# Moving the first expert's down product ahead of the second gather of slots, with an earlier load and wider table operations

## The reference, cut to what matters

```python
def hierarchical_moe(h, w_group, b_group, w_expert, b_expert, w_gate, w_up, w_down):
    ...
    weights = (g_w * e_w).reshape(-1)
    expert = (g_idx * EXPERTS_PER_GROUP + e_idx).reshape(-1)
    order = jnp.argsort(expert)
    tok = order // EXPERT_TOPK
    xs = t[tok]
    sizes = jnp.bincount(expert, length=N_EXPERTS).astype(jnp.int32)
    hid = jax.nn.silu(lax.ragged_dot(xs, w_gate, sizes)) * lax.ragged_dot(xs, w_up, sizes)
    out = lax.ragged_dot(hid.astype(xs.dtype), w_down, sizes)
    out = out * weights[order][:, None].astype(out.dtype)
    y = jnp.zeros_like(t).at[tok].add(out.astype(t.dtype))
```

## Time and profile before

| what | value |
|---|---|
| times of three runs | 1330.54, 1327.62, 1325.86 us; median 1327.62 |
| profiled execution, span | 1325.6 us (which of the runs it was isn't given; the span is all that is known of its time) |
| PE (matmul) busy | 1143.6 us, 86% |
| DVE busy | 634.0 us, 48% |
| ACT busy | 412.5 us, 31% |
| q1, the loads of SP | 335.06 MB, 66.5% of 16 engines |
| the chain that ended last | PE 68%, DMA 22%, DVE 5%, ACT 3% |
| of it, waiting for in_w_up | 21% |

### The profile page before, as it was taken

One profiled execution on the slowest core, in us unless ns is written; L12 is line 12 of the kernel. 1 busy time (PEld: TensorE's weight loads), 2 busy tenths in 40 slices (PEclk: granted clock), 3 DMA queues, 4 the chain that ended last, 5 costly groups with the idle time before them and its releaser, 6 DMA issues.

```text
span 1325.6 us, 22956 instructions
## 1 busy us (share of the span) xinstructions
PE 1143.6 (86%) x9319; PEld 922.7 (70%) x9321; DVE 634.0 (48%) x997; ACT 412.5 (31%) x519; POOL 32.7 (2%) x71
## 2 busy tenths in 40 slices
PE   9999999999989899999899999778766668567666
PEld 8998999998968899999798898653322323223222
DVE  5787877775444555446445787452221112111213
ACT  3765333324474433335333665320000000000001
POOL 0000000000000000000000000000000000000000
PEclk9999999999999999999999999878888889788889
DMA  9666988873530865550754334689999999999996
GB/s 350 218 253 223 335 300 301 301 270 127 191 128 1 286 193 188 190 190 32 136 177 143 128 134 173 260 326 417 428 430 429 428 428 430 428 429 430 428 428 257
DMA packets 99400, 362.47 MB, mean 273 GB/s; under 512 B 4160, under 2 KB 51664, under 8 KB 84112
## 3 DMA queue, kind: packets, MB, share of 16 engines
q1 hardware_dynamic: 95216, 335.06, 66.5%
q0 software_dynamic: 3984, 26.50, 5.0%
q10 hardware_dynamic: 144, 0.10, 0.0%
HBM read 360.58 MB, written 1.06 MB: 273 GB/s over the span
## 4 chain that ended last, share of the span: by engine, by line
PE 68%; DMA 22%; DVE 5%; ACT 3%; issue 2%; SPq 0%; DVEq 0%; POOL 0%; POOLq 0%; ACTq 0%
DMA wbuf<-in_w_up 21%; PE ps L1737 19%; PE ps L1672 15%; PE ps L1647 9%; PE ps L2032 7%; PE ps L1638 3%; PE ps L1656 3%; PE ps L1910 3%; PE ps L2082 2%; PE ps L1617 2%; PE ps L2052 1%; DVE parts L1057 1%; PE ps L1806 1%; DMA wbuf<-in_lru_w_in 1%; ACT parts_f L689 1%
## 5 line engine op out<-in xcount | busy, mean ns | idle before, releaser
L1737 PE MATMUL ps<-big_parts,parts 128*128 128x256 f32 x2112 | 261.6, 285 | 5.6 <-DVE big_parts L1057 5.1
L1057 DVE TENSOR_TENSOR parts<-wbuf,parts 128x2048 fp32r<-128x2048 f32 x88 | 200.1, 2289 | 136.9 <-ACT parts L799 52.3
L1737 PEld LDWEIGHTS ps<-big_parts,parts 128*128 128x128 f32 x2112 | 258.2, 194 | 7.7 <-issue 5.8
L2032 PE MATMUL ps<-wbuf,big 128*32 128x256 f32 x2176 | 167.2, 474 | 107.5 <-DMA wbuf<-in_w_up 100.1
L2032 PEld LDWEIGHTS ps<-wbuf,big 128*32 128x32 f32 x2176 | 86.2, 135 | 202.7 <-issue 94.0
L1672 PE MATMUL ps<-big_parts,parts 128*128 128x256 f32 x1344 | 166.1, 283 | 1.1 <-DVE parts_f L1261 1.1
L1672 PEld LDWEIGHTS ps<-big_parts,parts 128*128 128x128 f32 x1344 | 163.3, 192 | 1.3 <-issue 1.3
L989 ACT ACTIVATE big<-ps 128x128 f32<-128x128 f32 x33 | 9.2, 278 | 421.3 <-PE ps L2032 421.3
L1564 DVE TENSOR_TENSOR big<-big,ps 128x128 f32<-128x128 f32 x33 | 9.5, 288 | 264.1 <-ACT big L989 264.1
L1647 PE MATMUL ps<-parts_f,parts 128*128 128x256 f32 x672 | 97.2, 284 | 0.0
L1647 PEld LDWEIGHTS ps<-parts_f,parts 128*128 128x128 f32 x672 | 87.9, 192 | 0.2
(11 more groups left out here) (313 smaller groups left out, 1343.7 us busy)
## 6 DMA issues: line engine op xcount, KB each, us to landing
wbuf<-in_w_down SPq DMA_DIRECT2D x32, 2048.0 KB, 38.0
wbuf<-in_w_gate SPq DMA_DIRECT2D x31, 2048.0 KB, 32.6
wbuf<-in_w_up SPq DMA_DIRECT2D x31, 2048.0 KB, 37.1
wbuf<-in_ffn_w_in SPq DMA_DIRECT2D x44, 1024.0 KB, 11.1
wbuf<-in_w_ada POOLq DMA_DIRECT2D x24, 1024.0 KB, 8.3
wbuf<-in_ffn_w_out SPq DMA_DIRECT2D x22, 1024.0 KB, 5.1
wbuf<-in_w_in SPq DMA_DIRECT2D x10, 2048.0 KB, 8.1
wbuf<-in_attn_w_qkv SPq DMA_DIRECT2D x6, 2048.0 KB, 8.6
```

The lines of the kernel that those rows point to most:

```text
L1057: nc.vector.tensor_tensor(lo, whole, hi.bitcast(F32), ALU.subtract).then_inc(done, 1)
L1737: ins = mm(ps[:, b, d * 256:(d + 1) * 256], w[pw][:, k, d * P:(d + 1) * P], h_part_of[px][:, k], start=(k == 0 and i == 0), stop=(k == KC ...
L2032: ins = mm(at, rows, gu_place[s][:, :, k, r * P:(r + 1) * P], start=(k == 0), stop=(k == KC - 1))
```

## The change

It takes the first expert's down product from behind the second gather to ahead of it, on TensorE, and its hidden product ahead of the tables on VectorE. TensorE's wait for spread_ev goes with it, and a wait for y_ev comes into the gather. The spread products are made inside the first gate and up product, behind k = 4 and k = 6, the first of them into bank 3. gate_tile gets a place of its own, and POOL loads it directly after turned_mod. The table of further windows is made in two operations with a table of constants (full_windows, over_full), and that of row numbers in three. The memset of the last slots goes behind the first expert. The descriptor scratch of the software DMA is set to 8192 bytes.

```diff
--- before.py
+++ after.py
@@ -52,8 +52,9 @@
 
 C_ID, C_AFTER, C_BEFORE, C_ONES, C_ROT, C_STICK, C_NEG = 0, 128, 256, 384, 512, 640, 1024
 C_IOTA = 1408
-C_ROW = C_IOTA + GRP
-N_CONST = C_ROW + 1
+C_ROWS = C_IOTA + GRP
+C_FULL = C_ROWS + SEQ // WIN
+N_CONST = C_FULL + SEQ // WIN - 1
 N_ROUTE = N_GRP + N_EXP
 
 
@@ -153,6 +154,8 @@
         ada = sb("ada", [P, 48])
         gain = sb("gain", [P, 2, KC])
         small = sb("small", [P, 400])
+        gate_tile = sb("gate_tile", [P, 512])[:]
+        over_full = sb("over_full", [P, N_EXP * (SEQ // WIN - 1)])[:]
         bias36 = sb("bias36", [P, N_GRP + N_EXP])
         info = sb("info", [1, 3 * N_EXP], I32)
         turned_mod = cols[:, R_CW:R_CW + 2 * KC]
@@ -169,7 +172,8 @@
         minus_ones = cst[:, C_STICK + P:C_STICK + 2 * P]
         negm = cst[:, C_NEG:C_NEG + 384]
         iota8 = cst[:, C_IOTA:C_IOTA + GRP]
-        row_no = cst[:, C_ROW:C_ROW + 1]
+        row_of_window = cst[:, C_ROWS:C_ROWS + SEQ // WIN]
+        full_windows = cst[:, C_FULL:C_FULL + SEQ // WIN - 1]
 
         def flat(lo, n):
             return big[:, lo:lo + n]
@@ -231,7 +235,6 @@
 
             return h2_high[:, :, q // 2 * P:(q // 2 + 1) * P].rearrange("t k p -> t p k")[:, (q % 2) * (P // 2):(q % 2 + 1) * (P // 2)]
 
-        gate_tile = flat(10752, 512)
         final_row = wbuf[:, 2 * EXPERT:2 * EXPERT + D].rearrange("p (h f) -> p h f", h=2)
         part_logits = flat(5120, SEQ)
         zero_half = big_half[:, 2 * 512:2 * 512 + 512]
@@ -599,16 +602,13 @@
                 pool.dma_start(mod_dram[v].rearrange("(k p) -> p k", p=P), at, allow_slow_non_contiguous=True).then_inc(mod_stored, 16)
             pool.wait_ge(mod_stored, 48)
             pool.dma_start(turned_mod.rearrange("p (v k) -> p v k", v=2), mod_dram[0:2].rearrange("v (p k) -> p v k", k=KC)).then_inc(mod_turned, 16)
+            for h in range(2):
+                pool.dma_start(gate_tile[h * HALF_ROWS:(h + 1) * HALF_ROWS], mod_dram[2:3, h * 512:(h + 1) * 512].to_broadcast([HALF_ROWS, 512])).then_inc(gate_in, 16)
 
             pool.wait_ge(av_done, PAIRS)
             pool.dma_start(w_route, a["w_route"].rearrange("p (k n) -> p k n", k=KC)).then_inc(route_in, 16)
             pool.wait_ge(x_ready, 4 * 6)
             pool.dma_start(slot_no, a["slot_numbers"]).then_inc(slotno_in, 16)
-
-            pool.wait_ge(mod_stored, 48)
-            pool.wait_ge(spread_pe, 2)
-            for h in range(2):
-                pool.dma_start(gate_tile[h * HALF_ROWS:(h + 1) * HALF_ROWS], mod_dram[2:3, h * 512:(h + 1) * 512].to_broadcast([HALF_ROWS, 512])).then_inc(gate_in, 16)
 
             pool.wait_ge(info_ready, 1)
             n_more = pool.value_load(info[0:1, N_EXP:N_EXP + 1], min_val=0, max_val=SEQ // WIN - 1)
@@ -979,7 +979,7 @@
             nc.scalar.activation(first_silE, ps[:, 0, 0:P], ACT.Silu).then_inc(silu_done[0], 1)
             act.wait_ge(pick_ready, 2 * TC)
             act.wait_ge(spread_pe, 1)
-            nc.scalar.activation(slot_bc, ps[:, 1, :], ACT.Identity, bias=1.0).then_inc(spread_ev, 1)
+            nc.scalar.activation(slot_bc, ps[:, 3, :], ACT.Identity, bias=1.0).then_inc(spread_ev, 1)
             act.wait_ge(spread_pe, 2)
             nc.scalar.activation(weight_bc, ps[:, 2, :], ACT.Copy).then_inc(spread_ev, 1)
 
@@ -1529,23 +1529,29 @@
             ins.then_inc(spread_ready, 1)
 
             link(V.tensor_tensor(sm(32, 32), sm(32, 32), sm(START, 32), ALU.subtract))
-            link(V.tensor_scalar(sm(96, 32), sm(32, 32), float(WIN), None, ALU.is_gt))
-            for w in range(2, SEQ // WIN):
-                link(V.scalar_tensor_tensor(out=sm(96, 32), in0=sm(32, 32), scalar=float(w * WIN), in1=sm(96, 32), op0=ALU.is_gt, op1=ALU.add))
+            over_of = over_full.rearrange("p (e w) -> p e w", e=N_EXP)
+            link(V.tensor_tensor(over_of, sm(32, 32).unsqueeze(2).to_broadcast([P, N_EXP, SEQ // WIN - 1]),
+                                 full_windows.unsqueeze(1).to_broadcast([P, N_EXP, SEQ // WIN - 1]), ALU.is_gt))
+            link(V.reduce_sum(sm(96, 32), over_of, AX_X))
             V.tensor_copy(info[:, 32:64], small[0:1, 96:128]).then_inc(info_ready, 1)
             pick_half(1)
             link(V.tensor_tensor_scan(sm(128, 32), cst[:, C_ONES:C_ONES + 32], sm(96, 32), 0.0, ALU.mult, ALU.add))
             link(V.tensor_tensor(sm(128, 32), sm(128, 32), sm(96, 32), ALU.subtract))
             V.tensor_copy(info[:, 0:32], small[0:1, 0:32])
             V.tensor_copy(info[:, 64:96], small[0:1, 128:160]).then_inc(info_ready, 1)
-            for w in range(SEQ // WIN):
-                V.tensor_scalar(row_slot_t[:, w * N_EXP:(w + 1) * N_EXP], sm(START, 32), row_no, float(w * WIN + 1), ALU.add, ALU.add)
-                ins = V.tensor_scalar(row_used[:, w * N_EXP:(w + 1) * N_EXP], sm(32, 32), float(-w * WIN), row_no, ALU.add, ALU.is_gt)
-            link(ins)
-            link(V.tensor_tensor(row_slot, row_slot_t, row_used, ALU.mult))
+            dve.wait_ge(silu_done[0], 1)
+            V.tensor_tensor(first_hidE, first_silE, ps[:, 0, P:2 * P], ALU.mult).then_inc(hid_done[0], 1)
             V.memset(yE[0], 0.0).then_inc(y_ev[0], 1)
             V.memset(comb[0], 0.0).then_inc(comb_ready[0], 1)
-            V.memset(xs[:, :, SLOTS:], 0.0).then_inc(rows_end, 1)
+
+            def by_window(v):
+                return v.rearrange("p (w e) -> p w e", e=N_EXP)
+
+            every = [P, SEQ // WIN, N_EXP]
+            rows = row_of_window.unsqueeze(2).to_broadcast(every)
+            V.tensor_tensor(by_window(row_slot_t), sm(START, 32).unsqueeze(1).to_broadcast(every), rows, ALU.add)
+            link(V.tensor_tensor(by_window(row_used), sm(32, 32).unsqueeze(1).to_broadcast(every), rows, ALU.is_ge))
+            link(V.tensor_tensor(row_slot, row_slot_t, row_used, ALU.mult))
 
             def rest_of_window(q, count, at):
                 dve.wait_ge(hidT_pe[q], count + 1)
@@ -1564,8 +1570,6 @@
                 V.tensor_tensor(hidE, silE, ps[:, 0, P:2 * P], ALU.mult).then_inc(hid_done[q], 1)
                 rest_of_window(q, count, at)
 
-            dve.wait_ge(silu_done[0], 1)
-            V.tensor_tensor(first_hidE, first_silE, ps[:, 0, P:2 * P], ALU.mult).then_inc(hid_done[0], 1)
             dve.wait_ge(spread_ev, 2)
             dve.wait_ge(gate_in, 32)
             dve.wait_ge(info_ready, 2)
@@ -1574,6 +1578,7 @@
                 dve_window(1, w, nc.s_assert_within((w + 1) * N_EXP, 0, SEQ // WIN * N_EXP - 1, skip_runtime_bounds_check_because="w + 1 is less than the windows of a whole sequence"))
                 dve.wait_ge(more_done, w + 1)
             rest_of_window(0, 0, 0)
+            V.memset(xs[:, :, SLOTS:], 0.0).then_inc(rows_end, 1)
 
             with dve.Fori(1, N_EXP) as e:
                 n_more, before_more = more_windows(dve, e)
@@ -2037,10 +2042,11 @@
             for k in range(KC):
                 pe.wait_ge(gather_ev, k + 1)
                 ins = gate_up_product(k, xs[:, k, 0:WIN], 0)
+                if k in (4, 6):
+                    q = k // 2 - 2
+                    pe.wait_ge(spread_ready, 1)
+                    mm(ps[:, 3 - q, :], ones, spread[:, q], start=True, stop=True).then_inc(spread_pe, 1)
             ins.then_inc(first_gu, 1)
-            pe.wait_ge(spread_ready, 1)
-            for q in range(2):
-                mm(ps[:, 1 + q, :], ones, spread[:, q], start=True, stop=True).then_inc(spread_pe, 1)
             pe.wait_ge(zero_ready, 1)
             for b in range(4, 8):
                 mm(ps[:, b, :], zero_half[:, 0:P], zero_half, start=True, stop=False, skip_group_check=True)
@@ -2110,18 +2116,17 @@
                 pe.wait_ge(comb_ready[1], 2 * w + 2)
                 combine(1).then_inc(more_done, 1)
             nc.tensor.nop().then_inc(gu_done[0], 1)
+            pe.wait_ge(spread_ev, 2)
+            down_part(0, 0, 0, 1, first_hidE)
             pe.wait_ge(pick_ready, 2 * TC)
             for k in range(KC):
-                if k == 2:
-                    pe.wait_ge(spread_ev, 2)
-                if k == 6:
-                    pe.wait_ge(hid_done[0], 1)
+                if k == 4:
+                    pe.wait_ge(y_ev[0], 2)
                 b = (3, 1, 2, 0)[k // 2]
                 for i, (rows, c) in enumerate(((rows_high, 0), (rows_high, 1), (rows_low, 0), (rows_low, 1))):
                     ins = mm(ps[:, b, k % 2 * 256:(k % 2 + 1) * 256], rows(k, c), pick[1][:, c], start=(i == 0), stop=(i == 3))
                 ins.then_inc(gather_pe, 1)
             pe.wait_ge(gather_ev, 2 * KC)
-            down_part(0, 0, 0, 1, first_hidE)
             pe.wait_ge(info_ready, 2)
             with pe.Fori(0, (N_EXP - 2) // EXPERT_SLOTS) as j:
                 for i in range(1, EXPERT_SLOTS + 1):
@@ -2152,7 +2157,8 @@
     causal = np.where(i[None, :] <= i[:, None], 0.0, NEG)
     table[:, C_NEG:C_NEG + 384] = np.concatenate([causal, np.zeros((P, P)), causal], axis=1)
     table[:, C_IOTA:C_IOTA + GRP] = np.arange(GRP)
```

(5 more changed lines are left out.)

## The result

The changed kernel is slower: a median of 1333.98 us in 20 runs against 1327.53 us in 20 runs of the kernel before; the ratio of the two kernels, in which two disturbed executions of the changed kernel (1380 and 5278 us) don't count, is 1.0035, with a 95% interval of 1.0019 to 1.005, so +4.6 us (2.5 to 6.6). The three runs shown ahead of the prediction had nearly the same median of before (1327.62). The profiled execution after has a span of 1332.5 us, and its own time is 1334.26. The span is 6.9 us longer than the span of before. Two causes have to be kept apart in that: 4.5 us of it are there when G3 is issued (879.85 against 875.33), and 2.4 us come after (1332.5 - 879.85 = 452.6 against 1325.6 - 875.33 = 450.3).

What follows compares the result with a forecast made beforehand. The last 460 us were taken as bound by the weight stream and its holes. Old hole -2.9, gate_tile's bytes -0.8 and new hole +0.8 gave -2.9 us: from the median 1327.62 to 1324.7, range 1321.5 to 1329.9.

Steps and rivals of the forecast that it cites:

- G3: Load of expert 3's gate and up weights; its issue was forecast to stay at 875.3 us, with 0.1 either way.
- the old hole: Gap in the weight stream from 888.5 to 891.4 us, ahead of D3's bytes; forecast to close, 2.9 us gained.
- Part 1: gate_tile's loads moved far ahead of the experts: 0.8 us gained, at most 1.3, as their bytes leave the weight stream.
- Parts 2 and 3: Tables in fewer operations, and spread products inside the first product: nothing gained, with 0.1 us either way for the latter.
- Part 4: First expert's down product ahead of the gather: D3 issued earlier, 2.9 us gained, then 0.8 lost to a new hole.
- new hole of 0.8 us: Stream empty between D3's end at 892.6 and G4's bytes at 893.4; 0 if steps overlap, 2.5 at half clock.
- G4: Load of expert 4's gate and up weights, forecast to be issued at 891.8 us, with bytes from 893.4.
- D3: Load of expert 3's down weights, forecast to be issued at 880.7 us, at latest 882.4; before, at 889.78.
- I take the full clock: First expert's down product on TensorE, assumed at the 2.4 GHz level: 1.93 us, against 3.64 at half clock.
- G5: Load of expert 5's gate and up weights, forecast issued at 907.0 us, before at 909.65; no more than 0.5 lost.
- (c): Rival: VectorE's 7.79 us wait was its branch, not gate_tile, and moves with it: net +6.3, 1333.9 us; chance 0.07.
- (a): Rival: TensorE pays a code or clock stall at expert 1, priced at 4.03 us: net +1.1, 1328.7 us; chance 0.13.

Runs made afterwards that it cites:

- e1: Kernel before with only gate_tile loaded early, plus the smaller DMA scratch that makes room: ratio 0.9999 (0.9979 to 1.002), 445.8 us from G3 to the end.
- e8: Repeat of e1, the kernel before with only the early gate_tile load: ratio 0.9982 (0.996 to 1.0005), 446.4 us from G3 to the end.
- e10: Third run of e1, the kernel before with only the early gate_tile load: ratio 0.9982 (0.9963 to 1.0002), 446.4 us from G3 to the end.
- e3: Changed kernel with gate_tile's loads late again, behind spread_pe, in their own place: ratio 1.0037 (1.0017 to 1.0057).
- e2: Changed kernel with the first down product back behind the second gather: ratio 1.0004 (0.9978 to 1.0029), 445.8 us from G3 to the end.
- e11: Repeat of e2, the changed kernel with the down product back behind the gather: ratio 0.9972 (0.9955 to 0.9989), 446.1 us from G3 to the end.
- e9: Changed kernel again, unaltered, for a second profile: ratio 1.0029 (1.0012 to 1.0046), 453.7 us from G3 to the end.
- e4: Changed kernel with 26 more matmuls of zeros, 10 ahead of the down product and 16 behind the gather: ratio 1.0042 (1.0022 to 1.0062).
- e5: Kernel before with early gate_tile load, short tables and SP's release for G3 directly behind the first gate and up product: ratio 0.9983 (0.9962 to 1.0004).

## Why the prediction was wrong, point by point

I forecast 1324.7 us and 2.9 us less than before, with 1321.5 to 1329.9 as the range; it is 1333.98, 4.6 us more by the ratio.

**What bounds the kernel** was right: over the thirteen profiles of the table the stretch to the end goes with the stream's missing time, to 1 or 2 us, and the old hole and its cause (gate_tile, late) were as read. Undoing only that wait removed it in e1, e8 and e10.

**Part 1** was priced at 0.8 us, and the closing of the hole, 2.9 us, was booked under part 4. The early load does both by itself: alone it takes 3.9 to 4.7 us off the stretch (450.3 and 450.5 against 445.8, 446.4 and 446.4), a little more than the 3.7 of the two terms together. The whole time shows some 2 us of it. So the gain was right in its cause, and none of it needed the new order. The early loads landed after 3.0 us at most. The formula of the Trainium skill (DMA: Bandwidth & Descriptors, Anatomy of one DMA), 2.3 us for 128 KB, is 0.4 to 0.7 us short of the early loads, and the same loads took up to 9.1 us beside G3 in the profile of before and 5.4 in e3, where it doesn't hold.

**Parts 2 and 3** were costed at nothing, and at the end e2 and e11 show nothing against the gate load alone.

**Part 4** has the step that failed: "A **new hole of 0.8 us**", from "G4 is issued at 891.8", 16.5 us after G3. It was 21.1 and 21.0, and the hole 6.3 us. Part 4 as a whole stands in the sum with a gain of 2.1 us (-2.9 + 0.8); against the same kernel with the old order (e2, e11) it costs 6.5 to 7.9 us of the stretch. D3's issue was put at 5.4 us after G3 and came at 7.3 and 6.9. The terms, in the first profile:

- the copy: forecast 3.0 us after G3 (878.3), measured 3.2.
- "I take the full clock" for the down product, 1.93 us: it took 3.64, and 3.31 in e9. The clock fell in TensorE's pause ahead of it (2.46 us idle; the windows of 882 and 884 have 0.62 and 0.50), though I had the row of 0.66 and 0.50 beside me and named this as a bound. 1.7 us.
- the gather 5.06 instead of 4.01, its first part at the lower clock. 1.05 us.
- from ScalarE's last copy (893.15) to expert 1's product (895.42), 2.3 instead of 2.0. The two reads are in view:

```profile
L464 PEldq TENSOR_LOAD <-info x1: 319/319/319, 893.4 to 893.4; - x1
L465 PEldq TENSOR_LOAD <-info x1: 310/310/310, 894.2 to 894.2; - x1
```

- expert 1's product 5.35 instead of 3.7, and 6.51 in e9: TensorE had been idle for 3.3 us, and the clock went down again, in the first profile within the product (1.00 at 894 to 896, 0.54 at 896 to 898), in e9 ahead of it. 1.65 us.

With 0.2 for the copy and 0.3 for the reads these add up to 4.9 us, 0.3 more than the 4.6 between 16.5 and 21.1, which the rounded steps of the forecast leave. The lower clock has 1.7 + 1.05 + 1.65 = 4.4 of them; in e9 it has 4.3, divided otherwise (3.31, 4.08 and 6.51 us for the three). e4, in which the clock stayed up, bears this out up to expert 1's product. In the forecast every pause of TensorE was counted with its own length only, and most of the miss at G4 was the lower clock of the work behind the pauses. Then the hole: the bytes of D3 ran out at 896.3, 16.5 us after G3 and 0.8 earlier than I had worked out, so that it is 6.3 us wide, not 0.8. G5 added its own: expert 2's stop, 4.90 against 4.03, and a further lower clock brought some 2 us at 917 to 919, where I had allowed 0.5.

Of the **rivals**, (c) has the nearest number (1333.9) by a mechanism that didn't happen, and (a) the nearest mechanism: a hole before G4 that eats more than the gain. It was named as "a code or clock stall", priced with one code stop of 4.03 us, and ended at +1.1; it was the clock, and the hole was 5.5 us wider than forecast (6.3 against 0.8). The code stop that it expected at expert 1 was not there in the changed kernel, though a packet of code was loaded at 896.5, while the product ran; the stop appeared with the added instructions of e4. Expert 2 has a stop of 3.65 to 5.45 us in all thirteen profiles (in e4 just ahead of its product, in the others 5 to 7 matmuls into it), and the list of DMA queues has one packet of kind "instruction" inside each, 2.2 to 2.7 us before the work goes on. That agrees with the rule of the Trainium skill (Runtime: NRT & Kernel Launch, Instruction fetch mechanics), by which a taken branch to code outside the fetched window waits for a DMA; which branch it was, no row shows. In (c) VectorE's branch would have held the copy; the copy came 1.18 us after VectorE had the tables.

**The order itself** is what I judged too lightly. The gather at first looked like work that had to wait anyway; behind the down product it delays everything that expert 1 needs, and in front of it, it covers VectorE's tables, ScalarE's copies and the sequencer's reads. The new order bought 0.5 to 0.9 us of D3 (e1 has it at 7.8 and the changed kernel at 7.3, 6.9), and cost 9 us of G4 (12.1 against 21.0). About half of the 9 is the order by itself: with the clock up and no stop G4 would come at some 16.6 (the estimate of e4), 4.5 later than in e1, and most of the other 4.4 are the lower clock.

**What the stage leaves.** It accounts for +2.3 us in the first profile of the changed kernel and +3.4 in the second; the whole time says +4.6 (2.5 to 6.6). The 1.2 to 2.3 us between them are the open point of e9, and not much more than the interval allows.

**The measure.** I took the spread of the three runs shown as noise of some 2 us. It is 10.7 to 14.5 us in 29 to 35 runs of one kernel, and its steps are the clock's. The profiled execution of before was also not the fastest of the three, as I took it: a time lies 1.8 us above its span (1334.26 and 1332.5), so the span of 1325.6 belongs to a run of some 1327.4. The forecast went from the median and doesn't change.

**A better version** is in the table: the early load of gate_tile alone, 36 runs with a mean of 1326.5 us against 1328.8 of 119 runs of the kernel before and 1333.0 of 30 runs of the changed one; or the changed kernel with the old order (24 runs, 1327.0). Both are clearly better than the changed kernel. Against the kernel before they gain some 2 us, 0.15%, which only the runs taken together show: of the five ratios one is clear of 1, e11 with 0.9972 (0.9955 to 0.9989), and its twin e2 has 1.0004.

## What to carry to other kernels

When work is moved ahead of other work, write down the issue times of the next three loads and not only of the one that it frees: here the load that gained was 0.5 to 0.9 us better off than without the move, and the next one 9 us worse. Cost a pause of the matrix engine also with the lower clock that the work behind it may get. And where executions of one kernel fall in steps, compare the stage by itself, from one of its events to the end, before the whole time is blamed on the change.

## What the runs showed of the hardware

- Two loads of 128 KB through POOL's queue landed in 2.8 and 3.0 us at 661 us (2.7 to 3.0 in the other runs with the early load), 2.8 and 5.4 or 3.7 and 9.1 us beside the start of a stream of 4.2 MB: the same instruction, up to three times as long.
- The granted clock was at its lower level in three places ahead of the experts in some executions (15.71 against 14.05 us for 64 matmuls, 7.41 against 5.99 for 48) and in none of the three in others, with no difference in the program and the same pauses of TensorE. In the eleven experiments the first gather began at 861.99 to 862.39 us or at 865.26 to 869.53.
- A product of 64 matmuls that takes 3.66 us at the full clock took 5.35 and 6.51 us behind 3.3 us of idle time, with the granted clock at 0.50 for a part of it.
- Expert 2 stopped TensorE for 3.65 to 5.45 us in all thirteen profiles, with one packet of code (0.02 MB, kind "instruction") in each stop; 26 matmuls more brought a further stop of 2.76 us into expert 1's product, with such a packet in it too (e4).
- Making the stream's first load of the stage 2.1 us earlier (e5) did not bring the end forward. No run shows why.
